# Alternating the two sequences of a pair, column group by column group, in the sample tokens' paged attention

## The reference, cut to what matters

```python
kpast = cache_k[l][page_table].reshape(db, n_past, HA, 2, DQK)
vpast = cache_v[l][page_table].reshape(db, n_past, HA, DVA)
k_all = jnp.concatenate([kpast, ka], axis=1)          # and v_all
s = einsum('bqhcd,bkhcd->bhcqk', q, k) * DQK ** -0.5 - slopes * dist
p = softmax(where(mask, s, -inf));  w = p[:, :, 0] - lam * p[:, :, 1]
o = einsum('bhqk,bkhd->bqhd', w, v)
```

## Time and profile before

| | |
|---|---|
| median of 3 runs | 2119.85 us (2109.77 to 2121.35) |
| span of the profiled execution | 2116.2 us; no separate time of that execution is given, the median lies 3.65 us above its span |
| busy | PE 85%, PE weight load 42%, VectorE 63%, ScalarE 38%, GpSimd 35% of the span |
| DMA | 773.26 MB, mean 365 GB/s |
| paged attention | about 1489 to 1765 us |

### The profile page before, as it was taken

How to read it: one execution, slowest core, us unless ns; L and a number is a source line. 1 busy time by engine, 2 the same in 40 slices (tenths; PEclk the granted TensorE clock), 3 DMA queues, 4 the chain that set the end, 5 groups by cost and what they waited for, 6 DMA issues and landing times.

```text
span 2116.2 us, 20529 instructions
## 1 busy us (share of the span) xinstructions
PE 1790.3 (85%) x6195; PEld 890.4 (42%) x6195; DVE 1329.7 (63%) x3021; ACT 802.2 (38%) x2386; POOL 742.6 (35%) x638
## 2 busy tenths in 40 slices
PE   8899999889787888978888897969688899776877
PEld 3345454655344544534454453445223333442211
DVE  2661434379865689766678877557755554569554
ACT  2432212254463355445334636324323322323433
POOL 2210011044444444534434353443312233444442
PEclk9999999999999999989999999989889899988999
DMA  9682312599999999999999999999999999999998
GB/s 305 221 298 78 109 53 90 188 404 425 399 426 428 427 426 427 419 428 406 428 427 426 408 417 426 420 426 425 423 348 403 411 410 390 429 426 427 426 428 335
DMA packets 139817, 773.26 MB, mean 365 GB/s; under 512 B 14641, under 2 KB 23617, under 8 KB 62122
## 3 DMA queue, kind: packets, MB, share of 16 engines
q0 software_dynamic: 83232, 604.52, 68.4%
q1 hardware_dynamic: 52994, 160.12, 20.1%
q10 hardware_dynamic: 3480, 7.31, 1.0%
HBM read 755.91 MB, written 16.26 MB: 365 GB/s over the span
## 4 chain that ended last, share of the span: by engine, by line
PE 41%; DMA 26%; DVE 16%; ACT 8%; issue 5%; POOL 3%; SPq 1%; ACTq 0%; DVEq 0%; POOLq 0%
DMA sb_uv<-in_peer_uv,sb_eidx 22%; PE bank L2061 17%; DVE sb_uv L1666 7%; PE bank L1687 6%; PE bank L1962 3%; PE bank L2028 3%; PE bank L1996 2%; PE bank L1941 2%; POOL sb_uv L906 1%; DMA sb_zone<-in_cache_kT 1%; ACT sb_diag L1263 1%; ACT sb_ew L1256 1%; POOL sb_brs L849 1%; ACT L1252 1%; DMA pre_conv<-sb_raw 1%
## 5 line engine op out<-in xcount | busy, mean ns | idle before, releaser
L2061 PE MATMUL bank<-sb_uv,sb_diag 128*128 128x512 f32 (+1 forms) x1860 | 949.9, 647 | 246.0 <-ACT sb_diag L1263 239.2
L906 POOL DMA_INDIRECT sb_uv<-in_peer_uv,sb_eidx x576 | 672.3, 1167 | 1007.0 <-PE bank L2061 814.2
L1666 DVE CUSTOM_DVE_ANT_0 sb_uv<-sb_uv,sb_xn 128x1024 f32<-128x1024 f32 x576 | 697.3, 1220 | 267.0 <-DMA sb_uv<-in_peer_uv,sb_eidx 265.8
L2061 PEld LDWEIGHTS bank<-sb_uv,sb_diag 128*128 128x128 f32 (+1 forms) x1860 | 335.2, 195 | 728.4 <-ACT sb_diag L1263 381.2
L1252 ACT ACTIVATE sb_gel<-sb_h 128x1 f32<-128x1 f32 x576 | 116.1, 202 | 789.6 <-DVE sb_h L1666 785.6
L1687 PE MATMUL bank<-sb_w,sb_xnT 128*128 128x512 f32 (+1 forms) x560 | 261.6, 614 | 20.1 <-DMA sb_w<-in_w_sections 8.0
L1263 ACT ACTIVATE sb_diag<-sb_stay,sb_ew 128x128 f32<-128x128 f32 (+1 forms) x465 | 183.2, 394 | 43.7 <-ACT sb_ew L1256 1.1
L1640 DVE SCALAR_TENSOR_TENSOR sb_hres<-sb_uv,sb_ew,sb_hres 128x1024 f32<-128x1024 f32 x111 | 142.3, 1282 | 63.8 <-ACT sb_ew L1256 63.7
L1256 ACT ACTIVATE sb_ew<-sb_gel,sb_gate 128x1 f32<-128x1 f32 x576 | 169.7, 295 | 19.9
L2028 PEld LDWEIGHTS bank<-sb_rT,sb_zone 128*128 128x128 f32 x1280 | 155.3, 195 | 27.5 <-issue 27.5
L1687 PEld LDWEIGHTS bank<-sb_w,sb_xnT 128*128 128x128 f32 (+1 forms) x560 | 100.5, 188 | 142.1 <-issue 125.8
(11 more groups left out here) (321 smaller groups left out, 1530.6 us busy)
## 6 DMA issues: line engine op xcount, KB each, us to landing
sb_zone<-in_w_route SPq DMA_DIRECT2D x20, 2304.0 KB, 12.0
sb_zone<-in_w_mixer SPq DMA_DIRECT2D x10, 2048.0 KB, 12.2
sb_zone<-in_cache_kT SPq DMA_DIRECT2D x64, 256.0 KB, 7.0
sb_zone<-in_cache_v SPq DMA_DIRECT2D x64, 256.0 KB, 14.9
sb_w<-in_w_sections SPq DMA_DIRECT2D x28, 512.0 KB, 6.3
sb_uv<-in_peer_uv,sb_eidx POOLq DMA_INDIRECT x576, 13.6
sb_hres<-pre_conv SPq DMA_DIRECT2D x4, 1024.0 KB
sb_zone<-pre_conv SPq DMA_DIRECT2D x4, 1024.0 KB, 6.1
```

The source lines that it names most:

```text
L906: nc.gpsimd.indirect_dma_start(uv[:, m % RING, :], None, i["peer_uv"], bass.IndirectOffsetOnAxis(ap=eidx[:, t % 2, n:n + 1], axis=0)).then ...
L1666: nc.vector.tensor_tensor_reduce(out=uv[:, m % RING, 0:D], in0=uv[:, m % RING, 0:D], in1=xn2[:, t % 2, :], scale=1.0, scalar=0.0, op0=ALU. ...
L2061: ins = nc.tensor.matmul(bank[half][0:rows, :], lhsT=G["diag"][:, d % DIAGS, 0:rows], rhs=uv[:, m % RING, D + 512 * half:D + 512 * half + ...
```

## The change

Quarter q now holds pages 4(q//2) to 4(q//2)+3 of sequence q%2. Quarters 0 and 1 are thus half 0 of the pair's two sequences, and 2 and 3 are half 1. The four steps of scores become two, one for each half, and so do the four of values. Inside a step the matmuls of the two sequences stand in turn: they write to different rows of the same bank, and so use different columns of the PE array. The counts of matmuls, loads and bytes are the same. `s_ds` and `s_dpv` are incremented once for each half (2 for each pair instead of 4), and all waits on them are rewritten so. The steps come due where the odd quarter's step did: at 2 and 4 instead of 1, 2, 3, 4, and at 11.1 and 13.1 instead of 10.1 to 13.1. The new keys' matmuls come behind the cached ones and only in half 1.

```diff
@@ route_loads (SyncE)
-                            sp.wait_ge(s_dpv, 4 * (NPAIR - 1) + 2 * part + 2)
+                            sp.wait_ge(s_dpv, 2 * (NPAIR - 1) + part + 1)
@@ cache_loads (SyncE)
-                            n = (2 * p + q // 2) * NPG + 4 * (q % 2) + g
+                            n = (2 * p + q % 2) * NPG + 4 * (q // 2) + g
...
-                            sp.wait_ge(s_ds, 4 * p + q + 1)
+                            sp.wait_ge(s_ds, 2 * p + q // 2 + 1)
                         elif p:
-                            sp.wait_ge(s_dpv, 4 * (p - 1) + q + 1)
+                            sp.wait_ge(s_dpv, 2 * (p - 1) + q // 2 + 1)
@@ spread_queries, past_weights, past_out, mix_copy (ScalarE), past_bias (VectorE): 4 * ... becomes 2 * ..., as in
-                    act.wait_ge(s_dpv, 4 * (p + 1))
+                    act.wait_ge(s_dpv, 2 * (p + 1))
@@ past (TensorE)
-                    for q in range(4):
-                        yield past_at(p, 1 + q)
-                        r0, half = 64 * (q // 2), q % 2
-                        pe.wait_ge(s_kv[q], 16 + 64 * (2 * p + 1))
-                        if q == 0:
+                    for half in range(2):
+                        yield past_at(p, 2 + 2 * half)
+                        for seq in range(2):
+                            pe.wait_ge(s_kv[2 * half + seq], 16 + 64 * (2 * p + 1))
+                        if half == 0:
...
+                        for h in range(NH):
+                            for seq in range(2):
+                                ins = nc.tensor.matmul(bank[2 + half][64 * seq:64 * seq + 64, :].rearrange("p (g k) -> p g k", g=4), lhsT=Qd[:, h, seq, :],
+                                                       rhs=cache_quarter(2 * half + seq)[:, :, h * PAGE:(h + 1) * PAGE], start=h == 0, stop=h == NH - 1)
                         if half:
                             for h in range(NH):
-                                nc.tensor.matmul(bank[4][r0:r0 + 64, 0:NSAMP], lhsT=Qd[:, h, q // 2, :], rhs=kT[:, h, NPOS:TOK], start=h == 0, stop=h == NH - 1)
-                        for h in range(NH):
-                            ins = nc.tensor.matmul(bank[2 + half][r0:r0 + 64, :].rearrange("p (g k) -> p g k", g=4), lhsT=Qd[:, h, q // 2, :],
-                                                   rhs=cache_quarter(q)[:, :, h * PAGE:(h + 1) * PAGE], start=h == 0, stop=h == NH - 1)
+                                for seq in range(2):
+                                    ins = nc.tensor.matmul(bank[4][64 * seq:64 * seq + 64, 0:NSAMP], lhsT=Qd[:, h, seq, :], rhs=kT[:, h, NPOS:TOK], start=h == 0, stop=h == NH - 1)
                         ins.then_inc(s_ds, 1)
...
-                    for q in range(4):
-                        yield past_at(p, 10.1 + q)
+                    for half in range(2):
+                        yield past_at(p, 11.1 + 2 * half)
                         pe.wait_ge(s_dwc, 2 * (p + 1))
-                        pe.wait_ge(s_kv[q], 16 + 64 * (2 * p + 2))
+                        for seq in range(2):
+                            pe.wait_ge(s_kv[2 * half + seq], 16 + 64 * (2 * p + 2))
...
                         for g in range(4):
-                            at = 64 * (4 * half + g)
-                            ins = nc.tensor.matmul(out, lhsT=G["wT"][:, 0, at + cols.start:at + cols.stop], rhs=cache_quarter(q)[:, g, :], start=half == 0 and g == 0, stop=False)
+                            for seq in range(2):
+                                at = 64 * (4 * half + g) + 32 * seq
+                                ins = nc.tensor.matmul(outs[seq], lhsT=G["wT"][:, 0, at:at + 32], rhs=cache_quarter(2 * half + seq)[:, g, :], start=half == 0 and g == 0, stop=False)
                         if half:
-                            ins = nc.tensor.matmul(out, lhsT=G["wT"][0:NSAMP, 1, cols], rhs=vtok[0:NSAMP, PT, :], start=False, stop=True)
+                            for seq in range(2):
+                                ins = nc.tensor.matmul(outs[seq], lhsT=G["wT"][0:NSAMP, 1, 32 * seq:32 * seq + 32], rhs=vtok[0:NSAMP, PT, :], start=False, stop=True)
                         ins.then_inc(s_dpv, 1)
```

More of the change, by code:

```diff
@@ L1149, in spread_queries @@
                     if p:
-                        act.wait_ge(s_ds, 4 * p)
+                        act.wait_ge(s_ds, 2 * p)
                     for h in range(NH):
@@ L1166, in past_weights @@
                     if p:
-                        act.wait_ge(s_dpv, 4 * p)
+                        act.wait_ge(s_dpv, 2 * p)
                     nc.scalar.activation(G["wT"][:, 0, :], bank[5][:, :], ACT.Copy).then_inc(s_dwc, 1)
@@ L1183, in mix_copy @@
                         if n == PT:
-                            act.wait_ge(s_ds, 4 * NPAIR)
+                            act.wait_ge(s_ds, 2 * NPAIR)
                         if n + 1 == PT:
@@ L1518, in past_bias @@
                     yield past_at(p, 5.3)
-                    dve.wait_ge(s_ds, 4 * (p + 1))
+                    dve.wait_ge(s_ds, 2 * (p + 1))
                     if p == 0:
@@ L1950, in past @@
                     nc.tensor.matmul(bank[6][0:NSAMP, 0:64], lhsT=G["S"][:, 0, PAST:], rhs=G["fold"][:, :], start=True, stop=True).then_inc(s_dw, 1)
-                    for q in range(4):
-                        yield past_at(p, 10.1 + q)
-                        half, cols = q % 2, slice(32 * (q // 2), 32 * (q // 2) + 32)
-                        r0 = 64 * (p % 2) + 32 * (q // 2)
+                    for half in range(2):
+                        yield past_at(p, 11.1 + 2 * half)
                         pe.wait_ge(s_dwc, 2 * (p + 1))
-                        pe.wait_ge(s_kv[q], 16 + 64 * (2 * p + 2))
+                        for seq in range(2):
+                            pe.wait_ge(s_kv[2 * half + seq], 16 + 64 * (2 * p + 2))
                         if p:
                             pe.wait_ge(s_doc, p)
-                        out = bank[7][r0:r0 + 32, :]
+                        outs = [bank[7][64 * (p % 2) + 32 * seq:64 * (p % 2) + 32 * seq + 32, :] for seq in range(2)]
                         for g in range(4):
-                            at = 64 * (4 * half + g)
-                            ins = nc.tensor.matmul(out, lhsT=G["wT"][:, 0, at + cols.start:at + cols.stop], rhs=cache_quarter(q)[:, g, :], start=half == 0 and g == 0, stop=False)
+                            for seq in range(2):
+                                at = 64 * (4 * half + g) + 32 * seq
+                                ins = nc.tensor.matmul(outs[seq], lhsT=G["wT"][:, 0, at:at + 32], rhs=cache_quarter(2 * half + seq)[:, g, :], start=half == 0 and g == 0, stop=False)
                         if half:
-                            ins = nc.tensor.matmul(out, lhsT=G["wT"][0:NSAMP, 1, cols], rhs=vtok[0:NSAMP, PT, :], start=False, stop=True)
+                            for seq in range(2):
+                                ins = nc.tensor.matmul(outs[seq], lhsT=G["wT"][0:NSAMP, 1, 32 * seq:32 * seq + 32], rhs=vtok[0:NSAMP, PT, :], start=False, stop=True)
                         ins.then_inc(s_dpv, 1)
```

## The result

The changed kernel takes 2138.7 us (median of 5 runs, 2128.61 to 2142.38) against 2118.19 us before (5 runs, 2109.77 to 2121.35). The ratio is 1.0098, with a 95% interval of 1.0073 to 1.0124: slower by about 1%, where 2114 with a range up to 2126 was forecast. The profiled executions' spans are 2136.9 and 2116.2 us.

A forecast was written before the change was run, and what follows sets the result against it. DMA and PE were taken as nearly full, the end moving only by DMA waste removed in the attention stage. 7.5 - 1.5 = 6 us off the 2116.2 span gives 2110.2, plus 3.65 is 2113.9, written 2114; range 2100 to 2126.

The forecast's parts named there:

- What bounds the kernel: Paged attention stage: DMA and PE both nearly full; the end moves only by what DMA stops wasting there.
- PE time: Scores and values on TensorE: matmuls in turn overlap fully, saving 6.5 + 8.7 = 15 us a pair, 61 in four.
- New keys: L1939's matmuls, 8 records in 0.68 us: in turn they cost between half and all; taken as nothing saved.
- the 3.65 us between span and time: Term added to the forecast span of 2110.2 us, as the median of the runs lay that far above the span.
- The bound from rates: DMA from 1500 to 1800 us: its bytes need 284 to 289 us, so at most 11 to 16 us can be had.
- Waits made coarser: Half 1 of pair 0 waits for two quarters, its scores ending 0 to 5 us later; 1.5 us back in all.
- the 7.5 us that it was to win: DMA share gaps in the attention stage: 6.3 us in pair 1 and 1.2 us in the last pair.
- rival C: Coarser waits starve the DMA in each pair: a 4.3 us gap in each of four, 2131 us; chance 0.12.
- The sign it named: In the DMA profile, several stretches of ten us at a share under 0.8 would show starved DMA.
- A: DMA filled better than forecast, the whole 11 to 16 us saved: 2101 to 2109, say 2106; chance 0.25.
- B: PE alone bounds the attention stage: 61 us less, about 2059; chance 0.05.
- D: Nothing overlaps when matmuls stand in turn: PE as long as before, 2118 to 2124; chance 0.08.

The follow-up runs named there:

- e4: Changed kernel with the first 72 gathers of prompt tile 3 split, 8 KB rows fetched as two of 4 KB: 2106.73 us, ratio to before 0.9949.
- e12: Kernel before with gathers in two (4 KB pieces) and early first key loads: 2111.12 us, ratio to before 0.9968.
- e6: Kernel before with its four steps, only the order of the quarters as in the changed kernel: 2117.23 us, ratio to before 1.0003.
- e14: e6 with quarter 0 waiting also for quarter 1's data, and quarter 2 for quarter 3's: 2131.21 us, ratio to before 1.0063.
- e9: Changed kernel as it is, run again for comparison on another chip: 2136.66 us, ratio to before 1.0083.
- e5: Kernel before, attention unchanged, with the first 72 gathers of prompt tile 3 made in two of 4 KB a row: 2107.38 us, ratio to before 0.9947.
- e2: Changed kernel with each matmul of the cached values issued a second time, result unused: 2130.97 us, ratio to before 1.0075.
- e10: Changed kernel with the sequence as outer loop, so matmuls not in turn: 2136.72 us, ratio to before 1.0083.
- e8: Changed kernel with gathers in two (4 KB pieces) and the first pair's key loads due earlier: 2103.47 us, ratio to before 0.9942.
- e3: Changed kernel with GpSimd waiting for quarters 2 and 3 of the next pair's keys before gathering more rows: 2134.58 us, ratio to before 1.0068.

## Why the prediction was wrong

**What bounds the kernel: right in the main.** Over the kernels the time of the profiled execution goes roughly with the GB/s of one window: 414 and 410 at 2107 and 2111 (e4, e12), 402 at 2114 (e6), 388 at 2132 (e14), 380 and 383 at 2137 and 2139 (e9 and the changed kernel). It is not a close rule: e5 has 411 at 2116, e2 has 381 at 2126, e10 387 at 2136. PE's time had no such effect: e10 has 280 us of PE busy in that window and e9 254, and both take 2136.7; e5 has 319 and e4 276, at ratios of 0.9947 and 0.9949. That nothing but the DMA moved the end is more than these runs show.

**PE time: right, a little under.** L1962 was to fall to 28.8 us for four pairs and is at 29.9, with its last part from 8.3 to 4.2. L1941 was to be 28.8 and is 39.7, since five of its eight halves run after PE stood still, with the granted clock at half or rising from it, and take 5.3 to 6.3 us (the 5.77 us above, where 3.65 is the full rate). The prediction had no term for this. New keys, which I took at no saving, halved. About 51 us instead of 61. One small term of the sum was off as well: the 3.65 us between span and time compared two different executions; in the changed kernel one execution has 2138.7 against 2136.9, 1.8 us.

**The bound from rates: not contradicted.** "At most 11 to 16 us can be had" stands: e4, e5 and e8, with hardly a gap left, are 0.5 to 0.6% under before, 11 to 12 us, and e12, as full, 0.3%, 7 us. They fetch rows in other pieces, so they do not test the sum itself.

**"Waits made coarser": the step that failed.** I wrote that a later end of the first scores "costs nothing itself" and took "1.5 us back in all, between 0 and 5". The change gave back the 7.5 us that it was to win and 20 more. Already for pair 0 its size was off: the scores were to end 0 to 5 us later and ended 9.8 us later (1557.4 for 1547.6), about half of it because the last eight key loads went out 5 us later behind the store of prompt tile 2 (1513.6 for 1508.1). Beyond that, two things in the step were wrong. First, I followed the wait for two quarters only in pair 0; in pairs 1 to 3 I looked at when loads are issued and not at when two quarters land. They were issued as soon as before, and half 1 still waited 19.0, 17.0 and 3.6 us: PE was there 14 us sooner in pairs 1 and 2, and from the last load's issue to the landing it took 24.7, 25.5 and 18.0 us. That a fifth of the DMA brings two quarters in 25 us stood in the prediction under rival C. Second, that DMA is full during such a wait was taken as cover. It is, but what fills it is work that was already asked for. While PE waits no ring buffer and no quarter is given back, so the wait is paid afterwards in gaps like the one at 1690 to 1710. e14 shows with the waits alone that they cost time (1.0063) and that gaps follow them. That the same chain makes up the whole 20 us of the changed kernel is read from its trace.

**Rival C (0.12) is what happened**, by its mechanism: waits for two quarters with the slots queued behind, and gaps after pages and gathers have landed. It was priced at four gaps of 4.3 us and 2131; the window's share fell by 0.04 of 380, 15 us, its GB/s by 19 us, and the time was 2138.7. The sign it named came as well: four stretches of ten us under a share of 0.8 (from 1550, 1620, 1640 and 1690 on: 0.47, 0.78, 0.79, 0.72). My case against it, "pages left alone get the full rate, so the wait ends soon", overlooked that they are not alone until eight gathers have landed, 20 us later. A and B fail, since the DMA was filled worse, not better. D fails by the 3.65 us. With it, for these shapes, fails the rule of the Trainium skill (TensorE: Matmul & The Clock Gate, Part 3) that weight loads overlap only across row groups.

**What stays open:** how much of the cost is in the places and how much in their interplay with the waits, why early first keys helped pairs 2 and 3, and whether multiplying in turn is worth a few us once the gathers are in two (e8 against e12).

## What to carry to other kernels

Where the engine that takes the work and the DMA that brings it are both nearly full and feed each other through a few buffers, price a change by whether the next requests go out sooner or later, not by the engine's time: a step that waits for two loads instead of one holds back every release behind it, even if it then runs twice as fast. The two queues here shared the DMA by packets (3055 to 2922 in e4), so small-packet loads that gate the schedule starved beside large-packet ones; cutting the large ones to half the size made this kernel 0.3 to 0.6% faster than before, with matmuls in turn or without, where holding the gathers back (e3) did not. A full DMA during a wait is no proof that the wait is free.

## What the hardware showed unexpectedly

The packet counts of two busy queues were so nearly equal that packet size set the shares: 4 to 1 in bytes with 8 KB against 2 KB, 2.1 to 1 with 4 KB against 2 KB, with next to no loss of rate (412 GB/s from 1580 to 1620 in e4, 421 from 1600 to 1620 before). And fp32 matmuls in different groups of 64 or of 32 columns run at the full rate of each: 16 records in 3.65 us, 1.97 times as fast as one group.
